# One store for each block of u, and eight loads of it for each half of the scan

## The chip, the cores and the metric

The kernel runs on one core of one Trainium2 chip. The metric is the device time of one execution in microseconds (us). Three executions of the kernel before took 2443.58, 2450.1 and 2450.63 us; their median, 2450.1 us, is the time before.

## The reference

One layer of a streaming encoder is computed for a prompt of 1024 tokens and for eight sequences of 16 new tokens, 1152 token columns in all. What matters here is the first projection and the state-space branch that reads one part of it.

```python
h = _rmsnorm(x, g_pre) * (1.0 + scale) + shift
z = h @ w_in                       # 2048 -> 5712 columns
q, k, v, iq, ik, iw, za, u, zs = _split_cols(z)
...
# S5, for each of 64 groups of 16 channels, a state of 64 complex numbers:
bu = einsum('gpc,btgc->btgp', b_bar, u_blk)
hs = associative_scan(combine, (lam_bar, bu)) + decay * h
y  = einsum('gcp,btgp->btgc', cr, hs.real) - einsum('gcp,btgp->btgc', ci, hs.imag)
y_ssm = y + d_skip * u             # then GELU, GLU, gates, and the output projection
```

u is 1024 of the 5712 columns: 64 groups of 16 channels.

## The kernel before, in words

The program is a chain of stages, each a block with one instruction stream per engine: `prepare`, `project_in`, `gate_states`, `attend_prompt`, `attend_samples`, `project_out`. The change lies in `project_in` (L605 to L1511), which makes z transposed (columns on partitions, tokens along the row) and computes the S5 scan between the products.

**Blocks and slots.** The columns go by in 37 blocks of up to 128 (`BLOCKS`, L702): first the eight blocks of u, then the indexer's, the attention's and the gates'. Each block takes four slots, S = 4G + q; in slot q TensorE multiplies a quarter of the 2048 rows (`quarter`, L1340). Every weight piece is split into a high and a low part: SP loads `w_raw` (`load`, L775), ACT rounds `w_hi` (`high`, L912), DVE subtracts `w_lo` (`low`, L1136). At the end of a block ACT copies PSUM to `z_sb` (`evict`, L917) and stores it (`store`, L930).

**u on its way to the scan.** For the blocks of u, `evict` orders the tokens by step: token 8n + s is put at column s*144 + n of `z_sb`, for eight steps s and 144 columns n. `store` then writes each of them with eight transfers, one for each of its eight groups, to a DRAM tensor `u` laid out as step, channel, group, column (L937). All other blocks go to the DRAM tensor `zt` in one transfer (L940).

**The scan.** From slot SCAN = 36 on, which is the first slot of the block G = 9, the 64 groups are done in 16 halves of four groups, one for every two slots. In the even slots TensorE does `inputs(j)` (L1392: sixteen products of `uy` and `p_in`, at L1404), and three slots later `outputs(j)` (L1408). DVE and POOL do the recurrence in between, with the table `rot`. SP feeds this by `load_half(j)` (L802: `p_in`, then `uy`, then `rot`), issued in the even slot before that of `inputs(j)`; by `load_taps` (L822) in odd slots; and by `store_y` (L828) in odd slots, eight transfers, one for each step. The tile `uy` has three copies; `load_half(j)` for j of 3 and more waits until the stores of y of half j - 3 out of the same copy have landed (L812).

SP works this list in the order of the slots (L869 to L906): the next `w_raw` first, which waits until TensorE has done the slot's quarter (L779), then what the slot adds. In the slot S = 34 that is `load_half(0)` and behind it `load_states`, two loads of `state_rows`, which TensorE turns at the start of slot 36 (`turn_states`, L1385) ahead of `inputs(0)`. In slot 36 it is the last `store_taps` and behind it `load_half(1)`.

Of the kernel before, what the change touches and what calls it, by code (L numbers as in the profile page):

```python
# [15 lines left out]
P = 128  # L16
# [4 lines left out]
TOK = SEQ + DEC_B * DEC_S  # L21
# [9 lines left out]
GROUPS, CH, STATE = 64, 16, 64  # L31
PAIRS = GROUPS // 2
STEP = 8
NSTEP = TOK // STEP
# [3 lines left out]
COLS = 5712  # L38
Q0, K0, V0, IQ0, IK0, IW0, ZA0, U0, ZS0 = 0, 1024, 1280, 1536, 2560, 2624, 2640, 3664, 4688
# [565 lines left out]
def project_in(nc, io, out, keep, scr):  # L605
# [4 lines left out]
    with ExitStack() as ctx:  # L610
        signals = cleared_after(nc, ctx)

        def sb(name, shape, dt=F32):
            return ctx.enter_context(nc.sbuf_tensor(name, shape, dt))

        def sem(name):
            return new_signal(nc, signals, name)

        def sems(name, n):
            return [sem(f"{name}{i}") for i in range(n)]  # L620
# [17 lines left out]
        z_sb = sb("z_sb", [P, TOK])  # L638
# [15 lines left out]
        uy, p_in, rot, q_out, toep = [uy0, uy1, uy2], [p_in0, p_in1], [rot0, rot1], [q_out0, q_out1], [toep0, toep1]  # L654
# [22 lines left out]
        z_done, z_out, z_read = sem("z_done"), sem("z_out"), sems("z_read", NTC)  # L677
# [6 lines left out]
        p_land, rot_land, u_land, q_land, t_land = sems("p_land", 2), sems("rot_land", 2), sems("u_land", 3), sems("q_land", 2), sems("t_land", 2)  # L684
# [15 lines left out]
        zt = scr["zt"]  # L700
# [5 lines left out]
        N = len(BLOCKS)  # L706
        N_U = 8
        slices = [LATE_SLICES if IQ0 <= col < IQ0 + IDX_HEADS * IDX_DIM else SLICES for col, _, _ in BLOCKS]
        done_before = [sum(len(slices[B]) for B in range(G)) for G in range(N + 1)]
        read_before = [[sum(i < len(slices[B]) for B in range(G)) for G in range(N + 1)] for i in range(NTC)]  # L710
        stored_before = [16 * (8 * min(G, N_U) + max(G - N_U, 0)) for G in range(N + 1)]

        BUILD = 1
        SCAN = 4 * (BUILD + BATCHES)
# [59 lines left out]
        def _(sp):  # L774
# [27 lines left out]
            def load_half(j):  # L802
                if j == 0:
                    sp.wait_ge(w_ok, BATCHES)
                    sp.wait_ge(p_ok, 2 * BATCHES)
                    sp.wait_ge(p_T, 2 * BATCHES)
                if j >= 2:
                    sp.wait_ge(b_mm, j - 1)
                    sp.wait_ge(hist_ok, j - 1)
                    sp.wait_ge(hist_i_ok, j - 1)  # L810
                if j >= 3:
                    sp.wait_ge(y_out, 16 * STEP * (j - 2))  # L812
                js = slice(2 * j, 2 * j + 2)
                sp.dma_start(p_in[j % 2][:], scr["s5_in"][:, js]).then_inc(p_land[j % 2], 16)
                sp.dma_start(uy[j % 3][:], scr["u"].rearrange("s c g n -> (s c) g n")[:, 4 * j:4 * j + 4]).then_inc(u_land[j % 3], 16)
                sp.dma_start(rot[j % 2][:], scr["rot"][:, js]).then_inc(rot_land[j % 2], 16)

            def load_states():
# [50 lines left out]
            for S in range(4 * N):  # L869
                G, q = divmod(S, 4)  # L870
# [10 lines left out]
                if S == SCAN - 2:  # L881
                    load_half(0)
                    load_states()
                if S == SCAN:
                    sp.wait_ge(skip_ok, BATCHES)
                    load_half(1)
# [9 lines left out]
                if inputs_at(S + 2) is not None and inputs_at(S + 2) >= 2:  # L896
                    load_half(inputs_at(S + 2))
# [11 lines left out]
        def _(act):  # L909
# [20 lines left out]
            def store(G):  # L930
                col, m, _ = BLOCKS[G]
                i = len(slices[G]) - 1
                act.wait_ge(z_read[i], read_before[i][G + 1])
                c0 = slices[G][0][0]
                if G < N_U:
                    for g in range(8):
                        act.dma_start(scr["u"][:, :, 8 * G + g].rearrange("s c n -> c s n"),  # L937
                                      z_sb[CH * g:CH * g + CH].rearrange("c (s n) -> c s n", s=STEP)).then_inc(z_out, 16)
                else:
                    act.dma_start(zt[col:col + m, c0:], z_sb[0:m, c0:]).then_inc(z_out, 16)  # L940

            def copy_inputs(b):
                if b:
# [74 lines left out]
            for S in range(4 * N):  # L1018
                G, q = divmod(S, 4)
                if q == 0 and G:  # L1020
                    if G == 1:
                        evict(0, 0)
                        evict(0, 1)
                    evict(G - 1, len(slices[G - 1]) - 1)
                    store(G - 1)
# [23 lines left out]
                if q == 3 and G:  # L1049
                    for i in range(len(slices[G]) - 1):  # L1050
                        evict(G, i)
            evict(N - 1, len(slices[N - 1]) - 1)
            store(N - 1)
            act.wait_ge(z_out, stored_before[N])
            act.wait_ge(g_out, 16 * GATE_UNITS)
# [273 lines left out]
        def _(pe):  # L1329
# [62 lines left out]
            def inputs(j):  # L1392
                s = j % 2
                pe.wait_ge(p_land[s], 16 * (j // 2 + 1))
                pe.wait_ge(u_land[j % 3], 16 * (j // 3 + 1))
                if j == 0:
                    pe.wait_ge(p_copied, 2 * BATCHES)
                else:
                    pe.wait_ge(b_read, j)
                    pe.wait_ge(dec_copied, 2 * j)  # L1400
                for a in range(2):
                    for ri in range(2):
                        for g in range(2):
                            ins = M(ps_s[ri][64 * g:64 * g + 64, a * NSTEP:(a + 1) * NSTEP],  # L1404
                                    p_in[s][:, a, ri, 64 * g:64 * g + 64], uy[j % 3][:, 2 * a + g, :], start=True, stop=True)
                ins.then_inc(b_mm, 1)
# [79 lines left out]
            for S in range(4 * N):  # L1486
                G, q = divmod(S, 4)
# [1288 lines left out]

def hybrid_layer(nc, io, out):
    scr = {name: nc.dram_tensor(name, shape, F32, kind="Internal").ap() for name, shape in (
        ("zt", [COLS, TOK]), ("u", [STEP, CH, GROUPS, NSTEP]), ("s5_in", [P, PAIRS, 2, P]), ("s5_out", [P, PAIRS, 2, P]),
        ("rot", [P, PAIRS, 2, PSTEP]), ("toep", [P, GROUPS, P]), ("y", [1024, TOK]), ("gate_dram", [P, D_MODEL]))}  # L2780
    with ExitStack() as ctx:
        def sb(name, shape, dt=F32):
            return ctx.enter_context(nc.sbuf_tensor(name, shape, dt))

        keep = {"ident": sb("ident", [P, P])}
        keep["vecT_base"] = nc.sbuf_base
        keep["vecT"] = sb("vecT", [P, 72])
        keep["mod_base"] = nc.sbuf_base
        keep["mod"] = sb("mod", [P, 2 * KB, COND])
        keep["s5_tabs"] = sb("s5_tabs", [P, 5, PAIRS])  # L2790
        keep["maskb_base"] = nc.sbuf_base
        keep["maskb"] = sb("maskb", [P, P * (NT - 1) * NT // 2], BF16)
        with ExitStack() as early:
            early.enter_context(nc.sbuf_tensor("beside_maskb", [P, (BACK_BYTES - 2 * P * (NT - 1) * NT // 2) // 4], F32))
            keep["back_base"] = keep["maskb_base"]
            offset = keep["back_base"]
            keep["s5"] = {}
            for name, shape in S5_KEPT:
                keep["s5"][name] = nc.alloc_sbuf_tensor_at(name, shape, F32, offset=offset)
                offset += (4 * math.prod(shape[1:]) + 31) // 32 * 32  # L2800
            keep["back_free"] = offset
            keep["cT"] = early.enter_context(nc.sbuf_tensor("cT", [P, KB, 32], F32))

            keep["xT_base"] = (nc.sbuf_base + 31) // 32 * 32
            keep["xT"] = early.enter_context(nc.sbuf_tensor("xT", [P, KB, TOK], F32))
            keep["shared_base"] = (nc.sbuf_base + 31) // 32 * 32
            early.enter_context(nc.sbuf_tensor("beside_xT", [P, KB, TOK], F32))
            prepare(nc, io, keep, scr)
            project_in(nc, io, out, keep, scr)
        keep["ssm_base"] = (nc.sbuf_base + 31) // 32 * 32  # L2810
        keep["ssm_hi"], keep["ssm_lo"] = sb("ssm_hi", [P, 8, TOK], F32R), sb("ssm_lo", [P, 8, TOK], F32R)
        gate_states(nc, io, out, keep, scr)
        keep["attn_hi"], keep["attn_lo"] = sb("attn_hi", [P, 8, TOK], F32R), sb("attn_lo", [P, 8, TOK], F32R)
        with nc.sbuf_tensor("kT", [P, KV_HEADS, TOK], F32) as kT:
            keep["kT"] = kT
            with nc.sbuf_tensor("v_nat", [P, SEQ // P, KV_HEADS * HD], F32) as v_nat:
                keep["v_nat"] = v_nat
                attend_prompt(nc, out, keep, scr)
            attend_samples(nc, io, out, keep, scr)
        keep["gpost"] = sb("gpost", [P, D_MODEL // 2], F32R)  # L2820
        keep["sel"] = nc.alloc_sbuf_tensor_at("sel", [P, ROWS + P], F32R, offset=keep["mod_base"])
        project_out(nc, io, out, keep, scr)
# [17 lines left out]
```

## Time and profile before

| | |
|---|---|
| median of three runs | 2450.1 us |
| the profiled execution, its own time | 2450.92 us |
| its span, first to last instruction | 2449.1 us |
| TensorE busy | 2175.2 us |
| DVE, ACT, POOL busy | 1239.4, 733.3, 336.2 us |
| u stores issued by ACT | 64, of 72 KB each |
| u loads issued by SP | 16, of 288 KB each |

The page gives the busy time of each engine first and then the span in forty slices. `project_in` runs from about 215 us to 1494 us and the scan in it from about 465 to 720 us. TensorE's row of slices is close to nine tenths or more throughout that stage. A time in a timeline is counted from the span's start; "SPq" and "ACTq" are transfers that the SP and ACT sequencers issue, and their duration is the time that the issue takes, not the transfer.

### The profile page before, as it was taken

Reading aid. Unit: us, or ns where it says so; the run is one execution under the profiler, and the core shown is the slowest. Engines: PE = TensorE matmul, PEld = TensorE weight load, DVE = VectorE, ACT = ScalarE, POOL = GpSimd, SP = SyncE. Lnnn points to the kernel's source line nnn. Section 1 sums busy time; section 2 is a strip of 40 time slices with the busy share of each in tenths; the row PEclk is TensorE's granted clock in tenths of the full one; section 3 lists DMA queues with packets and bytes.
Section 4 is the critical chain, followed back from the end, with each engine's and each line's share of the span. In section 5 each row is a group of like instructions: output and inputs, shape, how many; then the busy total and the mean of one; then the engine's idle time right before and its main releaser. Section 6 shows DMA issues by size and latency. Waiting matters only on the chain. (4 is left out here: it accounts for less than half of the span.)

```text
span 2449.1 us, 33778 instructions
## 1 busy us (share of the span) xinstructions
PE 2175.2 (89%) x12705; PEld 1884.4 (77%) x12705; DVE 1239.4 (51%) x2493; ACT 733.3 (30%) x1434; POOL 336.2 (14%) x589
## 2 busy tenths in 40 slices
PE   4764999899999999999999995986897789998896
PEld 1223999888889999999999994884675468885774
DVE  7437323344423698888777653555664332123224
ACT  1114222211124333333332212336663212232231
POOL 1425322165510000000000000001000100003001
PEclk7777999999999999999999997997998589999997
DMA  8752445655543443333333335323102132226436
GB/s 276 267 206 82 97 113 117 150 163 177 175 124 84 101 109 86 82 91 86 89 96 86 90 78 168 101 69 115 38 18 53 58 83 77 77 75 190 117 91 176
DMA packets 337512, 277.45 MB, mean 113 GB/s; under 512 B 107418, under 2 KB 277346, under 8 KB 335562
## 3 DMA queue, kind: packets, MB, share of 16 engines
q1 hardware_dynamic: 308594, 239.03, 35.7%
q10 hardware_dynamic: 27872, 34.20, 4.3%
q0 software_dynamic: 896, 2.23, 0.3%
q8 instruction: 94, 1.54, 0.3%
q14 instruction: 56, 0.45, 0.1%
HBM read 215.18 MB, written 60.20 MB: 112 GB/s over the span
## 5 line engine op out<-in xcount | busy, mean ns | idle before, releaser
L1336 PE MATMUL ps_z<-h_hi,w_hi 128*128 128x384 f32 (+2 forms) x2032 | 699.0, 344 | 40.2 <-DVE h_lo L1148 38.8
L1338 PE MATMUL ps_z<-h_hi,w_lo 128*128 128x384 f32 (+2 forms) x2032 | 689.1, 339 | 0.0
L1337 PE MATMUL ps_z<-h_lo,w_hi 128*128 128x384 f32 (+2 forms) x2032 | 688.9, 339 | 0.0
L1336 PEld LDWEIGHTS ps_z<-h_hi,w_hi 128*128 128x128 f32 (+1 forms) x2032 | 380.8, 187 | 58.7 <-issue 43.1
L1338 PEld LDWEIGHTS ps_z<-h_hi,w_lo 128*128 128x128 f32 (+1 forms) x2032 | 380.8, 187 | 5.5
L1337 PEld LDWEIGHTS ps_z<-h_lo,w_hi 128*128 128x128 f32 (+1 forms) x2032 | 381.0, 188 | 5.0
L1139 DVE TENSOR_TENSOR w_lo<-w_raw,w_hi 128x512 fp32r<-128x512 f32 (+1 forms) x180 | 129.0, 717 | 380.0 <-ACT w_hi L915 379.2
L2618 DVE TENSOR_TENSOR o_lo<-o_raw,o_hi 128x512 fp32r<-128x512 f32 x128 | 90.2, 705 | 298.6 <-ACT o_hi L2580 298.2
L915 ACT ACTIVATE w_hi<-w_raw 128x512 fp32r<-128x512 f32 (+1 forms) x180 | 112.2, 628 | 332.3 <-DMA w_raw<-in_w_in 282.8
L2580 ACT ACTIVATE o_hi<-o_raw 128x512 fp32r<-128x512 f32 x128 | 81.1, 634 | 326.2 <-PE ps_out L2749 254.7
L1269 DVE MAX8 top<-score 128x8 f32<-128x1024 f32 (+5 forms) x192 | 171.1, 891 | 3.3
L1849 POOL TENSOR_TENSOR gate<-gate,za 128x1024 f32<-128x1024 f32 x8 | 18.7, 2341 | 1110.8 <-ACT gate L1882 1110.8
L1271 DVE MATCH_REPLACE8 score<-top,score 128x1024 f32<-128x1024 f32 (+5 forms) x192 | 168.1, 876 | 0.0
L992 ACT ACTIVATE rel<-ps_s 128x512 f32<-128x512 f32 (+5 forms) x192 | 80.7, 460 | 245.7 <-PE ps_s L1473 212.6
L2747 PE MATMUL ps_out<-o_hi,attn_hi 128*128 128x512 f32 x288 | 118.6, 412 | 21.6 <-DVE o_lo L2618 14.8
L928 ACT ACTIVATE z_sb<-ps_z 128x384 f32<-128x384 f32 (+2 forms) x127 | 76.3, 635 | 148.0 <-PE ps_z L1338 147.1
L1246 DVE SCALAR_TENSOR_TENSOR score<-rel,iw,score 128x512 f32<-128x512 f32 (+5 forms) x180 | 104.1, 581 | 31.3 <-ACT rel L992 20.5
L2747 PE MATMUL ps_out<-o_hi,ssm_hi 128*128 128x512 f32 x288 | 114.0, 396 | 6.0 <-DVE o_lo L2618 6.0
L2748 PE MATMUL ps_out<-o_lo,attn_hi 128*128 128x512 f32 x288 | 115.0, 399 | 0.0
L2749 PE MATMUL ps_out<-o_hi,attn_lo 128*128 128x512 f32 x288 | 114.5, 398 | 0.0
L2748 PE MATMUL ps_out<-o_lo,ssm_hi 128*128 128x512 f32 x288 | 113.1, 393 | 0.0
L2749 PE MATMUL ps_out<-o_hi,ssm_lo 128*128 128x512 f32 x288 | 113.0, 392 | 0.0
(410 smaller groups left out, 3114.1 us busy)
## 6 DMA issues: line engine op xcount, KB each, us to landing
w_raw<-in_w_in SPq DMA_DIRECT2D x176, 256.0 KB, 3.1
wada<-in_w_ada SPq DMA_DIRECT2D x32, 1024.0 KB, 9.1
o_raw<-in_w_out SPq DMA_DIRECT2D x128, 256.0 KB
wg<-in_w_ada SPq DMA_DIRECT2D x32, 512.0 KB, 5.0
zt<-z_sb ACTq DMA_DIRECT2D x28, 576.0 KB, 4.2
xs<-in_x_prompt SPq DMA_DIRECT2D x8, 1024.0 KB, 10.2
iq_raw<-zt SPq DMA_DIRECT2D x48, 128.0 KB, 3.3
u<-z_sb ACTq DMA_DIRECT2D x64, 72.0 KB, 2.2
```

The source lines that it names most:

```text
L915: A(w_hi[q][:, :, 0:m], w_raw[q][:, :, 0:m], ACT.Copy).then_inc(w_hi_ok[q], 1)
L1139: V.tensor_tensor(w_lo[q][:, :, 0:m], w_raw[q][:, :, 0:m], w_hi[q][:, :, 0:m].bitcast(F32), ALU.subtract).then_inc(w_lo_ok[q], 1)
L1246: V.scalar_tensor_tensor(to, rel[:, h2, 0:w], wgt, to, ALU.mult, ALU.add).then_inc(s_acc, 1)
L1269: V.max(top8[:], s).then_inc(top, 1)
L1271: V.match_replace(s, top8[:], s, CHOSEN).then_inc(top, 1)
L1336: M(to, w_hi[q][:, k, 0:m], h_hi[:, kk, cols], start=kk == 0, stop=False)
L1337: M(to, w_hi[q][:, k, 0:m], h_lo[:, kk, cols], start=False, stop=False)
L1338: return M(to, w_lo[q][:, k, 0:m], h_hi[:, kk, cols], start=False, stop=kk == KB - 1)
L2618: V.tensor_tensor(w_lo[:, kb % 2], w_raw[:, kb % 2], w_hi[:, kb % 2].bitcast(F32), ALU.subtract).then_inc(w_lo_ok, 1)
L2747: M(ps_o[i][:], hi[:, kb % NB, cols], w_hi[:, kb % 2], start=kb == 0, stop=False)
L2748: M(ps_o[i][:], hi[:, kb % NB, cols], w_lo[:, kb % 2], start=False, stop=False)
L2749: ins = M(ps_o[i][:], lo[:, kb % NB, cols], w_hi[:, kb % 2], start=False, stop=kb == KB - 1)
```

## The change

The eight blocks of u are stored like the others: one transfer for each block, from `z_sb` into its 128 rows of `zt`, in which a row keeps the order by steps. The DRAM tensor `u` is gone. Each half of the scan reads `uy` by eight transfers, one for each step: sixteen partitions, for each four runs of 144 numbers (576 bytes). `load_half(0)` has a wait more, for the stores of the eight blocks, and TensorE's wait for `u_land` counts eight transfers a half.

```diff
-        stored_before = [16 * (8 * min(G, N_U) + max(G - N_U, 0)) for G in range(N + 1)]
+        stored_before = [16 * G for G in range(N + 1)]
...
                     sp.wait_ge(p_T, 2 * BATCHES)
+                    sp.wait_ge(z_out, stored_before[N_U])
...
-                sp.dma_start(uy[j % 3][:], scr["u"].rearrange("s c g n -> (s c) g n")[:, 4 * j:4 * j + 4]).then_inc(u_land[j % 3], 16)
+                for s in range(STEP):
+                    sp.dma_start(uy[j % 3][CH * s:CH * s + CH],
+                                 zt[U0:U0 + 1024, NSTEP * s:NSTEP * s + NSTEP].rearrange("(g c) n -> c g n", c=CH)[:, 4 * j:4 * j + 4]).then_inc(u_land[j % 3], 16)
...
-                if G < N_U:
-                    for g in range(8):
-                        act.dma_start(scr["u"][:, :, 8 * G + g].rearrange("s c n -> c s n"),
-                                      z_sb[CH * g:CH * g + CH].rearrange("c (s n) -> c s n", s=STEP)).then_inc(z_out, 16)
-                else:
-                    act.dma_start(zt[col:col + m, c0:], z_sb[0:m, c0:]).then_inc(z_out, 16)
+                act.dma_start(zt[col:col + m, c0:], z_sb[0:m, c0:]).then_inc(z_out, 16)
...
-                pe.wait_ge(u_land[j % 3], 16 * (j // 3 + 1))
+                pe.wait_ge(u_land[j % 3], 16 * STEP * (j // 3 + 1))
```

The order of SP's instructions at the start of the scan, before: from the last store of `s_in` to the loads of the second half (L814 to L816 are `load_half`, L820 `load_states`, L800 `store_taps`).

```order
L787 DMA s_in<-pout 128x1024
L814 DMA p_in_1553<-s_in 128x512
L815 DMA uy_1552<-u 128x576
L816 DMA rot_1554<-rot 128x512
L820 DMA state_rows<-in_state_ssm_re 128x2x128
L820 DMA state_rows<-in_state_ssm_im 128x2x128
L782 DMA w_raw<-in_w_in 128x4x128 x2
L800 DMA toep<-taps 16x8x128 x8
L814 DMA p_in_1556<-s_in 128x512
L815 DMA uy_1555<-u 128x576
L816 DMA rot_1557<-rot 128x512
```

The same place on SP with the change (its L815, L817 and L819 are `load_half`, L823 is `load_states`).

```order
L787 DMA s_in<-pout 128x1024
L815 DMA p_in_1553<-s_in 128x512
L817 DMA uy_1552<-zt 16x4x144 x8
L819 DMA rot_1554<-rot 128x512
L823 DMA state_rows<-in_state_ssm_re 128x2x128
L823 DMA state_rows<-in_state_ssm_im 128x2x128
L782 DMA w_raw<-in_w_in 128x4x128 x2
L800 DMA toep<-taps 16x8x128 x8
L815 DMA p_in_1556<-s_in 128x512
L817 DMA uy_1555<-zt 16x4x144 x8
L819 DMA rot_1557<-rot 128x512
```

Seven transfers more stand ahead of `rot` and of both `state_rows` in the first half, and ahead of `rot` in the second; the order of the rest is the same.

SP in the middle of the scan, before: one odd slot (`w_raw`, `load_taps`, `store_y`) lies between two even ones.

```order
L831 DMA y<-uy_1552 16x4x144 x8
L782 DMA w_raw<-in_w_in 128x4x128
L814 DMA p_in_1556<-s_in 128x512
L815 DMA uy_1552<-u 128x576
L816 DMA rot_1557<-rot 128x512
L782 DMA w_raw<-in_w_in 128x4x128
L825 DMA q_out_1566<-s_out 128x512
L826 DMA toep_1567<-toep 128x512
L831 DMA y<-uy_1555 16x4x144 x8
```

The same rows with the change.

```order
L834 DMA y<-uy_1552 16x4x144 x8
L782 DMA w_raw<-in_w_in 128x4x128
L815 DMA p_in_1556<-s_in 128x512
L817 DMA uy_1552<-zt 16x4x144 x8
L819 DMA rot_1557<-rot 128x512
L782 DMA w_raw<-in_w_in 128x4x128
L828 DMA q_out_1566<-s_out 128x512
L829 DMA toep_1567<-toep 128x512
L834 DMA y<-uy_1555 16x4x144 x8
```

The loads of `uy` now have the shape of the stores of y, 16x4x144, and are as many.

## Rows read from the trace of the kernel before

**Rows 1.** Page: busy us (share) of the engines.

```profile
PE 2175.2 (89%) x12705; PEld 1884.4 (77%) x12705; DVE 1239.4 (51%) x2493; ACT 733.3 (30%) x1434; POOL 336.2 (14%) x589
```

**Rows 2.** Waits of PE, 250 to 470 us: us in total, times, longest.

```profile
PE ps_z L1336 <- DVE h_lo L1148: 2.0, 1, 2.0
```

**Rows 3.** Waits of PE, 720 to 1500 us.

```profile
PE ps_z L1336 <- ACT z_sb L928: 1.4, 1, 1.4
PE ps_w L1483 <- DMA wg<-in_w_ada: 0.4, 1, 0.4
```

**Rows 4.** Waits of PE in the scan, 470 to 720 us.

```profile
PE ps_s L1404 <- issue: 5.9, 1, 5.9
PE ps_s L1419 <- DMA toep<-toep: 1.0, 2, 0.5
PE ps_w L1389 <- DMA state_rows<-in_state_ssm_im: 0.7, 1, 0.7
```

**Rows 5.** DMA issues: xcount, KB each, median us from issue to landing.

```profile
zt<-z_sb ACTq DMA_DIRECT2D x28, 576.0 KB, 4.2
...
uy<-u SPq DMA_DIRECT2D x16, 288.0 KB, 3.9
```

**Rows 6.** Line L937: ns of one issue, min/median/max.

```profile
L937 ACTq DMA_DIRECT2D u<-z_sb x64: 309/454/1311, 253.6 to 452.3; - x64
```

**Rows 7.** Line L831, the stores of y: us to landing.

```profile
DMA to landing us min/median/max: 1.8/2.2/4.3
```

**Rows 8.** Timeline of SP: start, us, transfer; two sets of stores of y.

```profile
520.72 4.74 SPq L831 DMA_DIRECT2D y<-uy  x8
...
575.58 3.73 SPq L831 DMA_DIRECT2D y<-uy  x8
```

**Rows 9.** Timelines of SP and PE at the first half.

```profile
465.26 1.03 SPq L815 DMA_DIRECT2D uy<-u  x1
...
467.40 0.46 SPq L820 DMA_DIRECT2D state_rows<-in_state_ssm_im  x1
...
471.38 0.66 PE L1389 MATMUL ps_w<-ident,state_rows 128*128 128x128 f32 x4 [0.67 <-DMA state_rows<-in_state_ssm_im]
```

**Rows 10.** Timelines of SP and PE at the second half and the slot behind.

```profile
485.01 0.71 SPq L815 DMA_DIRECT2D uy<-u  x1
...
489.18 2.19 PE L1404 MATMUL ps_s<-uy,p_in 128*64 128x144 f32 x16 [5.90 <-issue]
491.30 0.74 PE L1336 MATMUL ps_z<-h_hi,w_hi 128*128 128x448 f32 x1
...
497.89 0.38 SPq L782 DMA_DIRECT2D w_raw<-in_w_in  x1
```

**Rows 11.** Windows: busy us by engine, PEclk, DMA share, GB/s; two idle times of PE.

```profile
487.00:489.00 2.00, 0.00 (x0) 0.00 (x0) 1.11 (x3) 0.00 (x0) 1.69 (x7) 0.66 0.95 321
489.00:491.00 2.00, 1.82 (x16) 1.76 (x16) 0.00 (x0) 0.01 (x1) 1.69 (x10) 0.50 0.96 304
...
2207.00:2211.00 4.00, 0.52 (x3) 0.27 (x2) 2.06 (x9) 2.82 (x5) 0.00 (x0) 1.00 0.00 0
2211.00:2213.00 2.00, 2.00 (x7) 1.52 (x7) 0.28 (x1) 0.00 (x0) 0.00 (x0) 0.59 0.53 89
```

**Rows 12.** Timelines of SP and PE, a half whose loads did not wait.

```profile
547.54 0.47 PE L1336 MATMUL ps_z<-h_hi,w_hi 128*128 128x448 f32 x1
...
552.70 0.40 SPq L782 DMA_DIRECT2D w_raw<-in_w_in  x1
...
553.69 0.43 SPq L815 DMA_DIRECT2D uy<-u  x1
...
559.82 1.20 PE L1404 MATMUL ps_s<-uy,p_in 128*64 128x144 f32 x16
```

**Rows 13.** Timelines of SP and PE, a half whose loads waited long.

```profile
582.77 0.43 SPq L815 DMA_DIRECT2D uy<-u  x1
...
587.43 1.20 PE L1404 MATMUL ps_s<-uy,p_in 128*64 128x144 f32 x16
```

**Rows 14.** SP's own waits, 470 to 720 us.

```profile
SPq L812 <- DMA y<-uy: 8.2, 9, 1.5
```

More of the change, by code:

```diff
@@ L2778, in hybrid_layer @@
     scr = {name: nc.dram_tensor(name, shape, F32, kind="Internal").ap() for name, shape in (
-        ("zt", [COLS, TOK]), ("u", [STEP, CH, GROUPS, NSTEP]), ("s5_in", [P, PAIRS, 2, P]), ("s5_out", [P, PAIRS, 2, P]),
+        ("zt", [COLS, TOK]), ("s5_in", [P, PAIRS, 2, P]), ("s5_out", [P, PAIRS, 2, P]),
         ("rot", [P, PAIRS, 2, PSTEP]), ("toep", [P, GROUPS, P]), ("y", [1024, TOK]), ("gate_dram", [P, D_MODEL]))}
```

## The prediction

> **What bounds the kernel now.** I read the page's busy times first: TensorE works 89% of the span and no other engine more than 51% [rows 1]. The next view is who waited for whom, taken for PE alone and by stretches, because the change touches two of them. In the blocks of u PE waits once, 2.0 us for `h_lo`, and never for a store or a weight [rows 2]. Behind the scan it waits 1.8 us in 780 us [rows 3]. So in this stage PE sets the pace: what is added to PE's waits is added to the end, and what other engines save gives nothing. In the scan PE waits three times over [rows 4]: 0.7 us for `state_rows`, 5.9 us ahead of one `inputs` (by the timeline the second half's, at 489.18 us), and 1.0 us for `toep`. The last view is the timeline of SP beside that of PE at three places: the first half [rows 9], the second [rows 10] and the middle of the scan [rows 12, 13]. The reader is to see there how long before its use each `uy` is issued.
>
> **What goes.** ACT issues 64 stores of u at 0.454 us each [rows 6], 29 us in all; 56 of them go, 25 us. I cost this at nothing: PE waits for no weight in that stretch [rows 2], so it is covered by PE's own work. If the cover were gone, it would be worth up to 25 us (a rival below). A block's store becomes one transfer of 576 KB as the other blocks have it, 4.2 us to landing [rows 5]; the next copy into `z_sb` comes three slots later, so this too costs nothing. The wait added to `load_half(0)` is for stores whose last issue began at 452.3 us [rows 6]; with 4.2 us to landing they are there by 457, and the first `uy` is issued at 465.26 [rows 9]. It costs nothing, and nothing queues behind it. The 16 loads of `uy`, 3.9 us to landing [rows 5], go as well.
>
> **What comes: the price of eight pieces.** No read of this shape is in the trace. The nearest row is the store of y: the same 16x4x144, also eight at a time, also on SP. Eight take 3.73 us to issue in one row and 4.74 in another [rows 8], and one lands 2.2 us after its issue, 1.8 to 4.3 [rows 7]. The eighth is issued at seven eighths, 3.3 to 4.1 us, so a whole `uy` is there 5.5 us after the first issue (5.1 to 8.4). I take 5.5 since both the faster set and the median landing are ordinary rows. Before, it was 3.9. Seven issues more cost SP about 3.3 us each time.
>
> **The terms.**
>
> 1. *First half.* SP issues `state_rows` behind `uy` and `rot`, the last at 467.40, and PE already waits 0.67 us for it [rows 9]. Seven more issues ahead put it off by their full length: 3.73 less the 1.03 of the one `uy` is 2.7; if the first piece is held up as that `uy` was (0.6 us more than an ordinary one), 3.3; with the slower set 4.3. If `state_rows` then land in 2.2 us like the small transfers and not in 3.9 like the large ones, 1.0 remains. I take 3.3, nearest to what SP does today; ends 1.0 and 4.3.
> 2. *The clock.* PE would now stand idle for 4.0 us there. In the wait before the second half the granted clock fell from 1.00 (2.4 GHz) to 0.50 (1.2 GHz) while PE stood idle, and PE restarted at 0.50 [rows 11]. After another idle time that left only 0.52 us of work in 4 us, it was 0.59 over the next two [rows 11]. What a restart at the lower level costs is seen in rows 10 and 12: `inputs` took 2.19 us against 1.20, and the quarter behind it, from its first product to SP's next `w_raw`, 6.59 us (491.30 to 497.89) against 5.16 (547.54 to 552.70). Together 2.4 us. I take 2.4, since both rows at idle times of this length show a fall; the other end is 0.
> 3. *Second half.* Its `uy` is issued at 485.01 and PE starts at 489.18, 4.2 us later, after a wait [rows 10]. With pieces it is 5.5 (5.1 to 8.4): 1.3 us more, 0.9 to 4.2. The first pieces are issued behind eight stores of taps, where one issue took 0.71 us [rows 10] and not 0.43, so I take 1.6. The clock is down there already, so no second fall is counted.
> 4. *Middle of the scan.* Where SP did not wait for y, `uy` is issued 6.1 us before its use (553.69 to 559.82) [rows 12]: 5.5 fits, at no cost. Where it waited long, 4.7 us remain (582.77 to 587.43) [rows 13]: 0.8 late. SP waited for y nine times, 8.2 us in all [rows 14], 0.9 each, which leaves 5.2 on average: 0.3 late, nine times, about 3 us. A stall here is returned in part, since the next quarter ends later while y has landed by then; I keep 3. Bounds: 0 when a piece lands in 1.8 us, since 5.1 is then under the average of 5.2; at 8.4 us 3.2 late nine times and 2.3 late four times, 38 us.
>
> `rot` is issued 3.3 us later, behind the pieces. DVE needs it only after `inputs`, 1.2 us later than PE needs `uy`, and its result is used three slots on; I cost it at nothing, and without that cover it would be 2 us a half at most. SP's next `w_raw` waits for PE's next quarter anyhow: 0.99 us from `w_raw` to `uy` (552.70 to 553.69) [rows 12] plus 3.73 for the pieces and 0.5 for `rot` is 5.2, and PE starts the next slot 7.1 us after that `w_raw`.
>
> **The sum.** 3.3 + 2.4 + 1.6 + 3 = 10.3 us, made against the profiled execution: 2450.9 + 10.3 = 2461.2. The median of the three runs is 0.8 us below that execution, so I predict 2460.4. A measurement of this kernel can tell a change from none at about 0.3%, 7.35 us.
>
> **Rivals.**
>
> *A. The issues hide, no change.* SP has idle time in every slot, and a piece may land early enough to fill it. For it: in the middle of the scan half of the loads have 6.1 us [rows 12]. Against it: at the first two halves PE is already waiting for SP's list [rows 9, 10]. It decides itself by whether the clock falls in the first wait and whether the mean late piece is late at all; without terms 2 and 4 it is 4.9 us, 2455; with the low ends 1.0 and 0.9 it is 2452. The Trainium skill (DMA: Bandwidth & Descriptors, "Issuing engines are not separate DMA queues") says that the sequencer's time to initiate a DMA is usually small beside the DMA itself; by that rule the eight issues would cost next to nothing and the terms 1 to 4 would be about 0. The rows speak against the rule at this size: eight issues of y take 3.73 us and one lands in 2.2. Chance 0.25.
>
> *B. Pieces land late throughout.* Eight reads of short runs stand behind `w_raw` and `p_in` in the same queue, and land in 3.3 us (between the median 2.2 and the maximum 4.3 of the stores) at the slower pace of 4.74 us: 7.4 us after the first issue. The middle then loses 2.2 us nine times and 1.3 four times, 25 us, of which the part returned by the next half's shorter wait for y is up to half: 12 to 25. With 4.3 + 2.4 + 3.2 at the start it is 22 to 35 us, 2472 to 2485. For it: the landing of y has such a maximum [rows 7]. Against it: its median. The Trainium skill (DMA: Bandwidth & Descriptors, "Rules for kernel authors") says to coalesce small transfers, and that under 64 KB one pays mostly overhead; the pieces are 36 KB. Read as a price of each piece one after the other, the rule would cost eight landings a half, but the rows of y show eight issued within 3.73 us without waiting for one another. Chance 0.2.
>
> *C. Faster: ACT was in the way.* In the blocks of u ACT's eight issues stand ahead of the next `w_hi`. If PE's weights were late by them, seven issues of 0.454 us less in eight blocks would give 25 us: 2425. It decides itself by whether PE waits behind a store; it does not in 200 us [rows 2]. Chance 0.05.
>
> The forecast itself has 0.5. That the change does not do what it says is excluded by the order of SP's instructions.
>
> **The numbers.** The forecast's own range, with the bounds of terms 1 and 3 and the middle between 0 and 8, is 2455 to 2468. For 8 times in 10 I add the upper half of A and the lower half of B: 2453 to 2474. Slower by over 0.3% begins at 2457.5. Of the forecast's 0.5 some 0.48 lies above, and with B it is 0.68. Within 0.3%: 0.25 of A and 0.02 of the forecast, 0.27. Faster: C, 0.05.
>
> **What would show it right or wrong.** In the profile of the changed kernel the wait of PE for `state_rows` should be 4 us, and the granted clock 0.50 at its end; the wait ahead of the second `inputs` some 7.5 us, with the eight pieces issued over 3.7 to 4.7 us; in the middle waits of PE at `inputs` of under 1 us in some of the halves, for `uy`; nothing new at the quarters in the blocks of u. Waits of 2 us in most halves would be rival B. A first wait under 2 us with the clock at 1.00, or no waits in the middle, would be rival A. I would be wrong in kind if PE's waits before 465 us were shorter than before, or if `rot` or a late `w_raw` stopped DVE long enough to reach PE.

## The result and the profile after

| | before | with the change |
|---|---|---|
| median, 7 runs each | 2449.14 us | 2458.46 us |
| lowest to highest | 2443.58 to 2450.63 | 2455.50 to 2461.26 |
| span of the profiled execution | 2449.1 us | 2456.7 us |

The ratio is 1.0041, with a 95% interval of 1.0029 to 1.0053: slower by 9.3 us at the medians (7 to 13 by the interval), clear of no change. The forecast was 10.3 us on top and 2460.4 us, with a range of 2453 to 2474.

The waits of PE in the scan of the changed kernel, 470 to 735 us (us in total, times, longest):

```profile
PE ps_s L1402 <- issue: 10.2, 4, 7.0
PE ps_w L1387 <- DMA state_rows<-in_state_ssm_im: 4.7, 1, 4.7
PE ps_s L1417 <- DMA toep<-toep: 1.6, 2, 1.4
```

They answer to [rows 4]: 16.5 us instead of 7.6, 8.9 more. The lines are moved by two; L1402 is `inputs`, L1387 the turning of `state_rows`. In the blocks of u, 250 to 470 us, where [rows 2] had 2.0 us, the same view of the changed kernel has no wait of PE at all. That is a matter of where the view begins: the stage starts at about 215 us, and from 200 to 465 us PE waits as long for `h_lo` as before (38.8 us, then 39.7 with the change):

```profile
PE ps_z L1336 <- DVE h_lo L1148: 38.8, 8, 32.2
...
PE ps_z L1334 <- DVE h_lo L1146: 39.7, 8, 32.3
```

The DMA issues (xcount, KB each, median us to landing), and the landing of the pieces of `uy` (line L817):

```profile
zt<-z_sb ACTq DMA_DIRECT2D x36, 576.0 KB, 4.1
uy<-zt SPq DMA_DIRECT2D x128, 36.0 KB, 2.0
DMA to landing us min/median/max: 1.8/2.0/3.6
```

So the read of this shape, which was priced from the stores of y [rows 7], lands as they do.

The timelines of SP and PE at the first half (start, us, line):

```profile
465.39 4.50 SPq L817 DMA_DIRECT2D uy<-zt  x8
...
470.88 0.47 SPq L823 DMA_DIRECT2D state_rows<-in_state_ssm_im  x1
...
475.48 1.12 PE L1387 MATMUL ps_w<-ident,state_rows 128*128 128x128 f32 x4 [4.66 <-DMA state_rows<-in_state_ssm_im]
476.52 2.19 PE L1402 MATMUL ps_s<-uy,p_in 128*64 128x144 f32 x16
```

In [rows 9] the one `uy` began at 465.26 and the last `state_rows` at 467.40, 2.1 us behind; now 5.5 us lie between them. The windows of the same stretch (busy us of PE, PEld, DVE, ACT, POOL; PEclk; DMA share; GB/s):

```profile
471.00:475.00 4.00, 0.00 (x0) 0.00 (x0) 1.16 (x3) 1.02 (x2) 0.00 (x0) 1.00 0.93 276
475.00:477.00 2.00, 1.52 (x8) 1.19 (x10) 0.37 (x2) 0.63 (x1) 0.00 (x0) 0.55 0.23 70
477.00:479.00 2.00, 2.00 (x18) 1.59 (x15) 0.76 (x6) 0.00 (x0) 0.00 (x0) 0.60 0.03 8
479.00:481.00 2.00, 2.00 (x12) 1.85 (x11) 2.00 (x7) 0.00 (x0) 0.00 (x0) 1.00 0.00 0
```

PE stands still, restarts at the lower clock (0.55 and 0.60 in these two windows), and has the higher one back by 479 us.

The timelines at the second half and the slot behind:

```profile
490.16 3.87 SPq L817 DMA_DIRECT2D uy<-zt  x8
...
495.65 2.19 PE L1402 MATMUL ps_s<-uy,p_in 128*64 128x144 f32 x16 [7.01 <-issue]
497.76 0.74 PE L1334 MATMUL ps_z<-h_hi,w_hi 128*128 128x448 f32 x1
...
503.52 0.38 SPq L782 DMA_DIRECT2D w_raw<-in_w_in  x1
```

PE starts 5.5 us after the first piece was issued, where it was 4.2 after the one load [rows 10]. In the middle three halves have a wait at `inputs`, 0.95, 0.43 and 1.82 us. The longest, by the timelines:

```profile
631.77 3.71 SPq L817 DMA_DIRECT2D uy<-zt  x8
...
637.10 1.20 PE L1402 MATMUL ps_s<-uy,p_in 128*64 128x144 f32 x16 [1.82 <-issue]
```

### The profile page after: what moved, and what is told of

Read it like the earlier page. It is cut to its first block and busy times, and to the rows that moved or that the text cites. A ratio compares the mean times of both kernels' runs of the same rounds, so it can differ in the third digit from the quotient of the medians.

```text
span 2456.7 us, 33835 instructions
## 1 busy us (share of the span) xinstructions
PE 2172.6 (88%) x12705; PEld 1884.3 (77%) x12705; DVE 1245.8 (51%) x2493; ACT 734.8 (30%) x1434; POOL 335.0 (14%) x589
## 5 line engine op out<-in xcount | busy, mean ns | idle before, releaser
L1334 PE MATMUL ps_z<-h_hi,w_hi 128*128 128x384 f32 (+2 forms) x2032 | 699.3, 344 | 40.8 <-DVE h_lo L1146 39.7
```

The source lines that it names most:

```text
L1334: M(to, w_hi[q][:, k, 0:m], h_hi[:, kk, cols], start=kk == 0, stop=False)
```

## The experiments

The theory: the price is the time that SP needs to issue seven transfers more, at the places where PE waits for what SP issues. The main rivals: the short runs or the rows of `zt` make the bytes slow; the store of u has a part; 128 reads cost wherever they are issued. Four runs went to one chip, four to another, three to a third; each ratio is to runs of the kernel before on the same chip, and has a 95% interval behind it. One trace is one execution, and executions of one kernel lie up to 7 us and more apart (2443.58 to 2450.63 before), so a trace is read for where the waits are.

**Eight loads, old layout.** The store of before, and only the loads by steps.

```diff
-                sp.dma_start(uy[j % 3][:], scr["u"].rearrange("s c g n -> (s c) g n")[:, 4 * j:4 * j + 4]).then_inc(u_land[j % 3], 16)
+                for s in range(STEP):
+                    sp.dma_start(uy[j % 3][CH * s:CH * s + CH], scr["u"][s][:, 4 * j:4 * j + 4]).then_inc(u_land[j % 3], 16)
...
-                pe.wait_ge(u_land[j % 3], 16 * (j // 3 + 1))
+                pe.wait_ge(u_land[j % 3], 16 * STEP * (j // 3 + 1))
```

> Only the loads are changed: u is stored by eight transfers a block into its own tensor as before, and each half reads it by eight transfers of 16 partitions, one for every step, in which a partition's four groups lie in one run of 2304 bytes and not in four of 576. Theory (the price is SP's time to issue seven transfers more): the same as the change, 9 us over before; wait for state_rows 4 to 5 us, the wait ahead of the second half 7 us, in the middle waits of under 2 us in a few halves. Rival (short runs and a worse layout in memory make the pieces land late): at most half of it, 0 to 4 us over before. Rival (the single store per block matters): its store is not changed here, so what is missing to 9 us would be its part.

Measured: 1.0028 (1.0013 to 1.0043), 2455.03 against 2447.66 us. The waits of PE in the scan:

```profile
PE ps_s L1405 <- issue: 8.4, 3, 7.1
PE ps_w L1390 <- DMA state_rows<-in_state_ssm_im: 4.2, 1, 4.2
```

The pattern of the change, with runs of 2304 bytes, but 7.4 us and not 9. Whether the 2 us between belong to the layout was left to a run beside the changed kernel on one chip:

> The changed kernel as it is, on the chip on which the next one runs. Theory: 9 us over before, wait for state_rows 4 to 5 us, ahead of the second half 7 us.

> Eight loads a half out of the old tensor, in runs of 2304 bytes, beside the changed kernel on one chip. Theory (SP's issue time alone is the price): level with the changed kernel within 2 us. Rival (the four runs of 576 bytes, or the longer rows of zt, cost something too): 2 to 4 us under the changed kernel.

Measured: the change 1.0048 (1.0033 to 1.0063), 2457.28 us; eight loads in the old layout 1.0045 (1.0033 to 1.0058), 2456.32 us; before 2446.22. They are one microsecond apart, with intervals that nearly coincide, and the pieces land in 2.0 us in both: no cost of runs and layout is seen, and the loads make the price or nearly all of it. The rival's lower end, 2 us, is not excluded by intervals of 3 to 4 us to either side. The waits of PE in the scan of this second profile of the changed kernel:

```profile
PE ps_s L1402 <- issue: 8.1, 4, 7.0
PE ps_w L1387 <- DMA state_rows<-in_state_ssm_im: 4.6, 1, 4.6
```

The two long waits are there again. What is left at `inputs` in the middle is 1.1 us, where the first profile had 3.2.

**One store, one load.** The store of the change, and one read of 288 KB for each half. It leaves out the order by steps in the read, so what it computes is not the layer.

```diff
-                for s in range(STEP):
-                    sp.dma_start(uy[j % 3][CH * s:CH * s + CH],
-                                 zt[U0:U0 + 1024, NSTEP * s:NSTEP * s + NSTEP].rearrange("(g c) n -> c g n", c=CH)[:, 4 * j:4 * j + 4]).then_inc(u_land[j % 3], 16)
+                r0, n0 = U0 + P * (j % 8), 4 * NSTEP * (j // 8)
+                sp.dma_start(uy[j % 3][:], zt[r0:r0 + P, n0:n0 + 4 * NSTEP].rearrange("p (g n) -> p g n", g=4)).then_inc(u_land[j % 3], 16)
...
```

> Only the store is changed: one transfer a block as with the change, and one transfer of 288 KB a half for reading. For this the scan reads u in a wrong order (rows of zt as they lie, without the division by steps), so its numbers are not u's; sizes and waits are the same. Theory (stores cost and give nothing, ACT is covered): the time of before within 2 us, wait for state_rows 0.7 us, ahead of the second half 5.9 us. Rival (fewer issues on ACT give something, and the loads cost more than the 9 us that are seen): 3 us or more under before. Rival (the store or the longer transfer costs): 3 us or more over before.

Measured: 1.0000 (0.9987 to 1.0012), 2447.20 us. ACT's 56 issues are worth nothing that can be seen, to some 3 us either way, where 25 us would be their whole length. One figure is off: the wait for `state_rows` is 2.6 us and not 0.7. The timelines show where it comes from:

```profile
464.08 0.47 SPq L822 DMA_DIRECT2D state_rows<-in_state_ssm_im  x1
...
470.10 0.65 PE L1386 MATMUL ps_w<-ident,state_rows 128*128 128x128 f32 x4 [2.64 <-DMA state_rows<-in_state_ssm_im]
```

From issue to use it is 6.0 us here, 4.0 in [rows 9], with the same list of SP ahead of it. What makes the 2 us is not shown: this run differs from that of before in the store of u and in the tensor that `uy` is read from.

**States first.** The changed kernel with two lines turned.

```diff
-                    load_half(0)
                     load_states()
+                    load_half(0)
```

> The changed kernel with one thing turned round: SP issues the two loads of state_rows ahead of the first half's loads and not behind them. Theory (what stands ahead of state_rows on SP is the first wait, and the lower clock follows from it): no wait for state_rows, but inputs of the first half now follow the loads of u, issued 0.9 us later than before the turn: the eighth piece lands at about 465.4 + 0.9 + 3.9 + 2.0 = 472.2 us, so PE waits under 1.5 us, the clock stays at 1.00, and 4 us of the 9 go: 5 us over before. Rival (the transfers, not their place, hold PE): the first wait stays at 4 us or more and the time at 9 us over before.

Measured: 1.0024 (1.0012 to 1.0037), 2452.86 us, 5.2 us over before. The wait for `state_rows` is gone, and at the first half is left:

```profile
469.52 1.20 PE L1402 MATMUL ps_s<-uy,p_in 128*64 128x144 f32 x16 [1.38 <-issue]
```

The sixteen products take 1.20 us, as at the higher clock. By the medians, turning two instructions gives back 4 of the 9 us; the interval here, 2.9 to 9.1 us over before, is wide. The profiled execution, 2447.93 us, is 4.9 below the median of the ten.

**Pieces on ACT.** The eight loads of a half are taken out of SP's `load_half` and issued by ACT. The wait for the stores of y, which stood ahead of them on SP, goes with them.

```diff
...
+            def load_u(j):
+                if j == 0:
+                    act.wait_ge(w_ok, BATCHES)
+                    act.wait_ge(p_ok, 2 * BATCHES)
+                    act.wait_ge(z_out, stored_before[N_U])
+                if j == 1:
+                    act.wait_ge(skip_ok, BATCHES)
+                if j >= 3:
+                    act.wait_ge(y_out, 16 * STEP * (j - 2))
+                for s in range(STEP):
+                    act.dma_start(uy[j % 3][CH * s:CH * s + CH],
+                                  zt[U0:U0 + 1024, NSTEP * s:NSTEP * s + NSTEP].rearrange("(g c) n -> c g n", c=CH)[:, 4 * j:4 * j + 4]).then_inc(u_land[j % 3], 16)
...
+                if inputs_at(S + 2) is not None:
+                    load_u(inputs_at(S + 2))
```

> The changed kernel with the eight loads of each half issued by ACT and not by SP, at ACT's place for the same slot. Theory (SP's list is the price): state_rows, rot and p_in are issued as early as before, so the wait for state_rows is 0.7 us again and the second half starts when p_in has landed, 1 to 2 us sooner than before; in the middle no waits at inputs. Time: 2 us under before to 1 over, if ACT's 128 issues of 0.43 us do not delay its own w_hi by more than the two slots it has. Rival (128 small reads cost by themselves, by landing or by what they take from w_raw and p_in): waits in the middle remain, 4 us or more over before. Rival (ACT becomes the one that is late, since it waits for y to land before its loads): new waits of PE for weights, 5 us or more over before.

Measured: 0.9998 (0.9988 to 1.0008), 2446.45 us. The same 128 reads, and nothing lost. The landing of the pieces, and PE's waits in the scan:

```profile
uy<-zt ACTq DMA_DIRECT2D x128, 36.0 KB, 2.9
...
PE ps_s L1411 <- DMA p_in<-s_in: 4.6, 1, 4.6
...
PE ps_s L1411 <- issue: 0.9, 3, 0.5
```

The wait for `state_rows` is gone, the second half starts when `p_in` lands, and the three waits in the middle are 0.9 us together, not none as expected. Both rivals, the reads by themselves and a late ACT, fall, although a piece lands in 2.9 us here and in 2.0 from SP. The run frees SP of the issues and of its wait for y (8.2 us in [rows 14]) at once, so in the middle of the scan it does not tell the two apart.

**Sixteen loads.** The cost doubled: sixteen transfers of 8 partitions out of the old layout.

```diff
...
+                for s in range(2 * STEP):
+                    sp.dma_start(uy[j % 3][8 * s:8 * s + 8],
+                                 scr["u"].rearrange("s c g n -> (s c) g n")[8 * s:8 * s + 8, 4 * j:4 * j + 4]).then_inc(u_land[j % 3], 16)
...
```

> The suspected cost doubled: u is stored as before, in its own tensor, and each half reads it by sixteen transfers of 8 partitions (18 KB each), the same bytes. Theory (SP's issue time is the price): fifteen issues more than before at about 0.47 us are 7 us. Wait for state_rows 8 us, ahead of the second half 10 to 11 us; in the middle the last piece lands 9 us after the first issue where 5 to 6 us are left, and SP's own work of two slots (5.3 for the odd one, 0.6 to 2 of waiting, 7.5 for the pieces, 1.3 for the rest) passes the 13.4 us that PE takes for them, so 2 to 4 us a half are lost in all thirteen: 45 to 70 us over before. Rival (the bytes and their landing are the price, the issues overlap): about as eight loads, 7 us over before, at most 15.

Measured: 1.0103 (1.0082 to 1.0124), 2472.66 against 2447.81 us: 25 us, more than the rival's 15 and about half of the theory's lower end. The waits of PE, and the issues at the first half and in the middle:

```profile
PE ps_s L1406 <- issue: 22.0, 14, 9.0
PE ps_w L1391 <- DMA state_rows<-in_state_ssm_im: 5.8, 1, 5.8
...
463.74 6.47 SPq L816 DMA_DIRECT2D uy<-u  x16
...
507.24 5.40 SPq L816 DMA_DIRECT2D uy<-u  x16
```

All thirteen halves of the middle wait now, but 1.0 us each (22.0 less 9.0, by thirteen) and not 2 to 4. Two things were mis-sized. A transfer half as long is issued faster, sixteen in 5.4 us where eight of 36 KB take 3.7. The second is argued and not tested: a stall ends the next quarter later, while y lands when it did, so part of it comes back. The direction is the theory's, the slope is not.

**Seven empty transfers.** The kernel before with seven transfers of 1 KB, memory to memory, between `uy` and `rot`. The first half also gets the wait for the stores of u, as in the change, and a wait for the seven stands ahead of a load behind the scan.

```diff
+                    sp.wait_ge(z_out, stored_before[N_U])
...
+                for i in range(STEP - 1):
+                    sp.dma_start(scr["junk"][j, i], scr["u"][0, :, 0, 16 * i:16 * i + 16]).then_inc(junk_out, 16)
                 sp.dma_start(rot[j % 2][:], scr["rot"][:, js]).then_inc(rot_land[j % 2], 16)
...
             def load_index():
+                sp.wait_ge(junk_out, 16 * 7 * HALVES)
```

> The kernel before with seven transfers of 1 KB, from memory to memory, on SP between the load of uy and that of rot; nobody waits for them, and uy is read by one transfer as before. Theory (what a transfer costs here is its issue on SP): state_rows is issued 2.3 to 3.3 us later, so the wait for it is 3 to 4 us, and the clock may fall for 1 to 2 us of work; the second half's uy stands ahead of them and waits as before, 5 to 6 us; in the middle rot lands 3 us later without PE seeing it. 3 to 5 us over before. Rival (bytes and landing of u are the price): 0 over before. Rival (a late rot or w_raw stops DVE and by it PE): 7 us or more over before, with new waits of PE in the middle.

Measured: 1.0051 (1.0037 to 1.0066), 2458.05 against 2446.22 us. The profiled execution of it, at 2452.64 us, is the lowest of its six. One set of issues on SP in it, and the waits of PE in the scan:

```profile
462.25 4.54 SPq L819 DMA_DIRECT2D junk<-u  x7
...
PE ps_w L1394 <- DMA state_rows<-in_state_ssm_im: 5.5, 1, 5.5
PE ps_s L1409 <- DMA p_in<-s_in: 4.9, 1, 4.9
PE ps_s L1424 <- DMA toep<-toep: 3.1, 6, 0.9
```

Transfers whose bytes nobody uses cost as much as the pieces of `uy`, so u's bytes are not needed for such a price. That the two prices are equal is partly chance, since they are made up of different waits. The size missed: 3 to 5 us were expected, and 7 or more was the sign of the rival with a late `rot`. Such a transfer takes 0.65 us to issue, not 0.45. DVE does wait for `rot`, nine times, 7.9 us in all, but PE is not seen to wait for DVE: its new waits in the middle are for `toep`, next on SP. The waits of PE are some 6 us more than before. The scan, from the end of the block ahead of it to the last `inputs`, takes 222.4 us (466.65 to 689.07) against 213.4 before (470.72 to 684.14), 9.0 more. This execution came to the scan 4.1 us sooner, which hides part of that in its time; what else keeps the median 5 us above it stays open.

**Two places reordered.** The same edit in the kernel before and in the changed one: `load_states` first, and in the scan's first slot the last `store_taps` and `load_half(1)` ahead of the next `w_raw`.

```diff
                 G, q = divmod(S, 4)
+                if S == SCAN:
+                    store_taps(BATCHES - 1)
+                    sp.wait_ge(skip_ok, BATCHES)
+                    load_half(1)
                 if G + 1 < N:
                     load(q, G + 1)
...
-                if 0 < G - BUILD <= BATCHES and q == 0:
+                if 0 < G - BUILD < BATCHES and q == 0:
                     store_taps(b - 1)
                 if S == SCAN - 2:
+                    load_states()
                     load_half(0)
-                    load_states()
-                if S == SCAN:
-                    sp.wait_ge(skip_ok, BATCHES)
-                    load_half(1)
```

> The kernel before, with two places of SP's list turned: the loads of state_rows ahead of the first half's, and in the scan's first slot the last stores of taps and the second half's loads ahead of the next w_raw, which waits for PE's quarter. Theory (SP's order is what PE waits for at the start of the scan, and the lower clock follows from the wait): the taps are ready at 473.6 us, so the second half's uy is issued at about 478.5 us and not at 485, and lands as PE ends its quarter; the wait of 5.9 us goes, and with it the slower inputs and quarter, 2.4 us, and 0.7 us for state_rows: 8 to 9 us under before. Rival (the wait ahead of the second half is for something else, as the chain of POOL and DVE behind the stores of taps): at most 2 us under before.

Measured: 0.9967 (0.9954 to 0.9980), 2440.79 against 2447.81 us. SP's list and PE at the second half:

```profile
473.43 4.52 SPq L800 DMA_DIRECT2D toep<-taps  x8
478.00 0.69 SPq L814 DMA_DIRECT2D p_in<-s_in  x1
478.73 0.74 SPq L815 DMA_DIRECT2D uy<-u  x1
...
482.42 1.20 PE L1405 MATMUL ps_s<-uy,p_in 128*64 128x144 f32 x16 [0.19 <-issue]
```

The wait of 5.9 us [rows 10] is 0.2, and `inputs` takes 1.20 us instead of 2.19. So it had been SP's order, and 7 us of it could be had (8 to 9 were expected).

> The changed kernel with the same two places of SP's list turned. Theory: what the eight loads cost at the start of the scan goes nearly whole, since PE no longer waits for what stands behind them: 1.4 us at the first half and under 1.5 us at the second remain, with the clock at 1.00, and about 3 us in the middle stay, since the order there is the same. 4 to 6 us over the reordered kernel before, 3 to 5 us under before. Rival (the eight loads cost what they cost wherever they stand): 9 us over the reordered kernel before, 0 against before.

Measured: 0.9982 (0.9974 to 0.9991), 2443.84 us, 3.0 us above the reordered kernel before. PE's waits at `inputs` are these:

```profile
PE ps_s L1403 <- issue: 4.4, 8, 1.3
```

1.3 and 1.0 us of them are at the first two halves, 2.1 in the middle. So by the medians the price of the eight loads falls from 9 to 3 us when `state_rows` and the second half's loads no longer stand where they did; between the two profiled executions it is 5.1 us (2446.81 and 2441.74), nearer to the 4 to 6 that were expected.

> The changed kernel with its eight loads issued by ACT, and the two places of SP's list turned. Theory: both prices go, the one of SP's eight issues and the waits that the kernel before has at the start of the scan: 8 to 10 us under before, and level with the reordered kernel before within 3 us. Rival (ACT's place in the first slots is too late for the second half, since it waits there for weights and for the block's end): the second half still waits 2 us or more, and it is 3 us or more behind the reordered kernel before.

Measured: 0.9960 (0.9948 to 0.9972), 2438.28 us, the lowest of all. What is left at `inputs`:

```profile
PE ps_s L1412 <- issue: 0.6, 2, 0.5
```

It beats both kernels; the 2.5 us to the reordered kernel before are within what the two intervals leave open.

## Why the prediction was right

The sign and the mechanism held, and the total too, though not each term. In the profiled execution, by its terms:

1. *First half*, 3.3 us. The wait for `state_rows` grew from 0.67 to 4.66, by 4.0. SP issued the eight pieces in 4.50 us against 1.03 for one `uy`, 3.5 more, and the landing was 0.6 longer. That SP's order is the cause is shown by turning it: the wait is gone, and by the medians 4 us with it.
2. *The clock*, 2.4 us. It fell, and the turning and the first `inputs` took 1.12 and 2.19 us instead of 0.66 and 1.20, 1.4 us together. The slower quarter that the term also counted did not come: the clock was back at 1.00 by 479 us. So this term was a microsecond too large, because the price was taken from a restart [rows 10] where the lower clock lasted through about half of the quarter (0.50 from 491 to 493 us, 0.63 to 495, then 1.00). The quarter behind the second half, in turn, took 5.76 us (497.76 to 503.52) and not 6.59, 0.8 us less than before.
3. *Second half*, 1.6 us. The wait went from 5.90 to 7.01, 1.1. The reading that a whole `uy` is there 5.5 us after its first issue is met here to a tenth; in the halves of the middle that waited it is 5.2, 5.3 and, where the eight took 4.74 us to issue, 6.3.
4. *The middle*, about 3 us. Three halves waited, 3.2 us in all; it was put as nine halves at 0.3. The few long waits lie where SP had waited for y: in the changed kernel ten times, 10.3 us, against nine and 8.2 [rows 14]. Waits for `toep` added 0.6 us (1.6 against 1.0).

Together 4.0 + 1.4 + 1.1 - 0.8 + 3.2 + 0.6 = 9.5 us. From the end of the block ahead of the scan (470.7 and 470.8 us) to the turning of the last states (721.31 and 730.85) the traces are 9.4 us apart, so the terms hold all of it in this pair of executions. The spans differ by 7.6; behind the scan, where nothing was changed, the changed kernel's execution is 1.9 us shorter.

The second profile of the changed kernel does not bear out the middle. At the start of the scan it agrees, with waits of 4.62 and 6.96 us. The third `inputs` and the last, before (first two lines) and in the second profile (last two):

```profile
505.00 1.20 PE L1404 MATMUL ps_s<-uy,p_in 128*64 128x144 f32 x16
...
684.14 1.20 PE L1404 MATMUL ps_s<-uy,p_in 128*64 128x144 f32 x16
...
512.21 1.20 PE L1402 MATMUL ps_s<-uy,p_in 128*64 128x144 f32 x16
...
691.35 1.20 PE L1402 MATMUL ps_s<-uy,p_in 128*64 128x144 f32 x16
```

From the one to the other it is 179.1 us in both, against 183.1 in the first profile; the two runs of eight loads in the old layout have 179.4 and 179.5. So the 3 us of term 4 are met by one trace of four, which is luck, and the price that all four show is that of the scan's start, 5.5 to 5.9 us up to the third `inputs`. In the three other traces the scan, from the block ahead of it to the last `inputs`, is 5.9 to 6.1 us longer than before, while the medians of the runs are 7.4 to 11.1 us up; where the rest lies stays open.

The errors of the terms also cancelled: the clock was put 1.0 us too high (1.8 with the quarter behind the second half) and the second half 0.5, the first half 0.7 too low. By its own bounds the forecast's range is 2454 to 2469 and not 2455 to 2468, which changes nothing; the 8 us for the middle in it are not worked out. The signs were met: a first wait of 4.7 us with the clock at 0.55 behind it, and 7.0 us ahead of the second `inputs`. One wait in the middle, 1.82 us, was over the 1 us that was named. PE's waits ahead of the scan were not shorter, when they are counted from 200 us on.

What was costed at nothing shows no cost: the store, by the run with one store and one load; the added wait, since `uy` follows `p_in` at once (465.39, by 465.01); and `rot`, which DVE is not seen to wait for in the change.

Rival A failed at the start of the scan, where SP's issues are not hidden; in the middle three of the four traces are nearer to it than to the forecast. The rule of the Trainium skill that it was weighed with (DMA: Bandwidth & Descriptors, "Issuing engines are not separate DMA queues") is that the sequencer's time is usually small beside the DMA itself. For one piece the rows are not far from that, 0.46 us of issue to 2.0 of landing; for eight it does not hold, since they are issued one behind the other, in 3.71 to 4.74 us, while their landings overlap. The same section of the Trainium skill says that several issuing engines save only the time of the issue. The run with the loads on ACT agrees, in that it gave back all of the 9 us, but it also moved SP's wait for y. Rival B failed by the landing, 2.0 us in the median. The rule of the Trainium skill on small transfers (DMA: Bandwidth & Descriptors, "Rules for kernel authors"), read as a price of each by itself, is not borne out: on ACT 128 of them cost nothing that is seen. Rival C failed: PE's waits ahead of the scan are what they were, 38.8 and 39.7 us, and the run with only the store changed is level with the kernel before. [rows 2], by which it was weighed, leave out the first 35 us of the stage.

## What to carry to other kernels

A transfer has a price on the engine that issues it, 0.34 to 0.65 us here, for 1 KB as for 36, and what stands behind it in that engine's list is put off by this; look for the first instruction behind it that a busy engine already waits for. Where a load is split, move ahead of it what is needed sooner, or issue the pieces from an engine with idle time. Here the first gave back 4 to 6 of the 9 us that the split costs, the second all of it. The cost of a stall is the wait and the slower work behind it, 1.4 us at the first half here and 2.4 at the second before, by how long the lower clock lasted in each.

## What the runs showed that was not expected

Issue time depends on the transfer: sixteen of 18 KB took 5.4 us (0.34 each), eight of 36 KB 3.7 (0.46), seven of 1 KB from memory to memory 4.5 (0.65). The landing of `state_rows`, with the same list of SP ahead of it, was 4.0 us in the kernel before and 6.0 in the run with one store and one load, and the cause is open. And the kernel before had 7 us to give at the scan's first slots, which [rows 10] had shown as a wait of PE without naming a cause.
